# Prompt attention with its keys stored by residue class of the token

## The chip, the cores and the metric

The kernel runs on one core of a Trainium2 chip, as one program. The metric is device microseconds of one execution, the median of three runs. In what follows TensorE is also PE (its weight loads are PEld), VectorE is DVE, ScalarE is ACT, GpSimd is POOL, and SyncE, which issues most of the transfers, is SP.

## The reference, cut to what matters

One layer of a decoder runs over a prompt of 2048 tokens and over 8 samples of 4 tokens. Its attention has 8 heads of 64. Three patterns (window, dilation d) = (128, 1), (512, 4), (2048, 16) are computed for every query, each over the keys at distances 0, d, 2d, ..., window, and merged by their softmax denominators. The prompt's part is:

```python
def dilated_band_attention(q, k, v, dil, n_back):
    n = s // dil; nb = n_pad // Q_BLOCK; z = b * dil          # Q_BLOCK = 128
    qs, ks, vs = to_sub(q), to_sub(k), to_sub(v)                # sub-sequence z holds tokens z, z+d, z+2d, ...
    kb, vb = blocks_with_prev(ks), blocks_with_prev(vs)         # [previous block, own block]
    scores = jnp.einsum('znqhd,znkhd->znhqk', qb, kb) * (HEAD_DIM ** -0.5)
    dist = qi + Q_BLOCK - ki
    valid = (dist >= 0) & (dist <= n_back) & (blk * Q_BLOCK - Q_BLOCK + ki >= 0)
    scores = jnp.where(valid[None, :, None], scores, -jnp.inf)
    lse = jax.nn.logsumexp(scores, axis=-1)
    p = jnp.exp(scores - lse[..., None])
    o = jnp.einsum('znhqk,znkhd->znqhd', p, vb)
```

The rest of the layer (modulated norms, the input projection, a state-space mixer, the attention of the samples over their caches, the output projection and a gated FFN) is not touched by the change.

## The kernel before

The stages run one after another, with a barrier between them: input projection, state space, prompt attention (lines 168 to 475, from about 641 to 981 us of the span), sample attention, mixing, FFN. Everything here is about the stage of the prompt's attention, `attention_stage`.

**Tiling.** The stage has 48 steps: 16 for each pattern, pattern 1 (d = 1), then 2 (d = 4), then 3 (d = 16). A step `n` takes one block of 128 queries of one residue class modulo d, with its own block of 128 keys and, where `has_prev(n)` is true, the block before it. That is so in 15 of the 16 steps of pattern 1, in 12 of 16 of pattern 2 (four classes of four blocks each) and in none of pattern 3 (16 classes of one block). A step is two halves `i = 2n + quad` of four heads each. All values are 32-bit floats.

**Where q and k lie.** In the first 16 steps the queries and keys of 128 consecutive tokens are loaded, turned on TensorE (line 312), and moved out of the PSUM bank into `qT` (by VectorE, line 421) and `kT` (by ScalarE, line 387). Both hold the head dimension on the partitions and the 2048 tokens in order along the row. The score matmul (line 327) picks its tokens with a step:

```python
first = (b + 1 - blocks) * QB * d + z
return slice(first, first + (blocks * QB - 1) * d + 1, d)
```

so neighbouring elements read are 1, 4 or 16 floats apart. The queries are the stationary operand (weight load of 128 columns, 64 partitions), the keys the moving one (128 or 256 columns). A half has four such matmuls, each recorded as two instructions, alternating between partitions 0 to 63 and 64 to 127.

**What follows a score.** VectorE scales, adds `mask` (128 x 256, zero in the band and -1e30 outside, built once on GpSimd, lines 266 to 270) and takes the row's bound (line 436); ScalarE takes exponentials, four instructions a half (line 394); TensorE turns the probabilities (line 339), 8 blocks with a previous block and 4 without; ScalarE and VectorE move them to `probsT` (387, 421); TensorE multiplies them with the rows of `v` (line 357), whose partitions are the keys of the block in order; ScalarE copies the result (402), TensorE turns it back (365), VectorE copies it into `o` (442), and GpSimd stores `o` (274).

**What sets the order.** Each engine runs its own written list and waits on semaphores. TensorE's loop over the halves is, for half i: turn the next queries (i odd) or keys (i even) while there are any; `scores(i)`; `back` (i odd); `probs(i-2)`; `values(i-3)`. VectorE's: move out turned queries (i odd), `maxima(i)`, its share of turned probabilities of i-2, the output (i odd). ScalarE's: move out turned keys (i even), `exps(i-1)`, its share of turned probabilities of i-2, `oT_out` (i even). The turned tiles (queries, keys, probabilities) take two PSUM banks in turn, in the order `turn_order`; TensorE may fill a bank again only when the tile before in that bank has been moved out (`free_turn_bank`). SyncE loads v two steps late (`V_LATE`) into a ring of four, gated by `valued`, and at the end of its list issues the first loads of the sample stage.

## Time and profile before

| what | us |
|---|---|
| median of 3 runs | 2994.49 |
| lowest and highest run | 2991.29, 2995.83 |
| the profiled execution's own time | 2997.85 |
| its span in the trace | 2996.1 |
| granted TensorE clock, mean of that execution | 0.966 of full |

Times inside the trace are microseconds from the start of the span. Busy time is the time in which an engine has an instruction under way, and of neighbouring instructions on TensorE the ends overlap the next ones' starts, so a group's length is best read from its start to the start of the next group. A count behind a name (x8) is a count of instructions merged into one row.

### The profile page before, as it was taken

What the parts mean: (1) busy time and instruction counts of PE and PEld (TensorE: products, weight loads), DVE (VectorE), ACT (ScalarE), POOL (GpSimd) and SP (SyncE); (2) the same over time, 40 slices, a digit from 0 to 9 for tenths busy, and PEclk for the clock granted to TensorE, in tenths of its full rate; (3) what the DMA queues carried; (4) which work ended last, traced back from release to release, by engine and by line L of the source; (5) the groups of instructions that cost most, each with busy time, mean ns of one, the idle gap of its engine ahead of it and who ended that gap; (6) DMA issues with size and microseconds to landing.
All of it is one profiled execution on the core that took longest, in us unless ns stands there. A gap on an engine that the chain in (4) does not pass through costs nothing.

```text
span 2996.1 us, 40303 instructions
## 1 busy us (share of the span) xinstructions
PE 2803.8 (94%) x15949; PEld 2272.1 (76%) x15949; DVE 1316.3 (44%) x2761; ACT 997.2 (33%) x2039; POOL 414.9 (14%) x556
## 2 busy tenths in 40 slices
PE   5899997989999777999599999999999999999997
PEld 3578876767777555887488888888888888999986
DVE  6446874656556327886233322333233332333321
ACT  3112221347768325665222212222122221223210
POOL 1207675420001000000000011000110001100011
PEclk8999998999999878999799999999999999999999
DMA  7663424733113855554755545556354654545421
GB/s 274 200 191 115 133 100 155 270 113 125 70 69 129 336 213 199 190 193 148 225 168 154 186 145 175 152 158 204 121 175 146 195 174 127 170 141 155 138 88 44
DMA packets 326421, 484.21 MB, mean 162 GB/s; under 512 B 22793, under 2 KB 229897, under 8 KB 317514
## 3 DMA queue, kind: packets, MB, share of 16 engines
q1 hardware_dynamic: 307168, 355.63, 36.6%
q0 software_dynamic: 18672, 125.85, 12.2%
q8 instruction: 127, 2.08, 0.3%
q14 instruction: 60, 0.49, 0.1%
q10 hardware_dynamic: 394, 0.16, 0.0%
HBM read 392.28 MB, written 155.95 MB: 183 GB/s over the span
## 4 chain that ended last, share of the span: by engine, by line
PE 51%; DMA 0%; POOL 0%; SPq 0%; DVE 0%; issue 0%; ACT 0%; POOLq 0%; DVEq 0%; ACTq 0%
PE f_ps_f L2249 33%; PE f_ps_f L2267 17%; DMA f_raw_f<-in_w_gate_dram 0%; POOL f_y_f L2220 0%; SPq L2161 0%; ACT f_ws_f L2281 0%; DVE f_tmp_f L2319 0%; DVE f_ws_f L2309 0%; POOL out_dram L2223 0%; POOL out_dram L2225 0%; DVEq L2318 0%; POOLq L2219 0%; POOLq L2217 0%; ACTq L2133 0%
## 5 line engine op out<-in xcount | busy, mean ns | idle before, releaser
L2249 PE MATMUL f_ps_f<-f_h_f,f_ws_f 128*128 128x512 f32 (+1 forms) x5280 | 1002.5, 352 | 27.1 <-DVE f_ws_f L2309 27.1
L2249 PEld LDWEIGHTS f_ps_f<-f_h_f,f_ws_f 128*128 128x128 f32 x5280 | 860.0, 188 | 169.1 <-DVE f_ws_f L2309 27.3
L2267 PE MATMUL f_ps_f<-f_ws_f,f_aT_f 128*128 128x512 f32 x2244 | 519.2, 393 | 1.0 <-DVE f_tmp_f L2319 1.0
L2309 DVE TENSOR_TENSOR f_ws_f<-f_raw_f,f_ws_f 128x1024 fp32r<-128x1024 f32 x264 | 315.9, 1224 | 416.9 <-ACT f_ws_f L2281 416.9
L2267 PEld LDWEIGHTS f_ps_f<-f_ws_f,f_aT_f 128*128 128x128 f32 x2244 | 422.0, 188 | 97.4 <-DVE f_tmp_f L2319 1.5
L2281 ACT ACTIVATE f_ws_f<-f_raw_f 128x1024 fp32r<-128x1024 f32 x264 | 268.5, 1048 | 421.3 <-PE f_ps_f L2267 394.7
L815 PE MATMUL p_out_ps<-p_w,p_hT 128*128 128x512 f32 x1632 | 387.1, 396 | 6.0 <-DVE p_qk L1063 3.7
L815 PEld LDWEIGHTS p_out_ps<-p_w,p_hT 128*128 128x128 f32 x1632 | 306.4, 190 | 79.9 <-issue 14.1
L2332 DVE TENSOR_TENSOR f_tmp_f<-f_sl_f,f_ps_f 128x512 f32<-128x512 f32 (+1 forms) x110 | 64.6, 588 | 562.0 <-PE f_ps_f L2249 561.6
L2297 ACT ACTIVATE f_aT_f<-f_tmp_f 128x512 fp32r<-128x512 f32 (+1 forms) x110 | 60.7, 552 | 520.6 <-DVE f_tmp_f L2332 520.6
L1852 PE MATMUL c_ps_w<-c_wout,c_mT 128*128 128x512 f32 (+1 forms) x816 | 195.6, 397 | 1.9 <-ACT c_wout L1880 0.9
L1852 PEld LDWEIGHTS c_ps_w<-c_wout,c_mT 128*128 128x128 f32 (+1 forms) x816 | 147.6, 183 | 43.2 <-ACT c_wout L1880 2.5
L394 ACT ACTIVATE a_probs<-a_probs,a_o 128x256 f32<-128x256 f32 (+1 forms) x384 | 171.7, 450 | 4.5 <-DVE a_o L436 4.5
L436 DVE CUSTOM_DVE_ANT_0 a_probs<-a_s_ps,a_mask 128x256 f32<-128x256 f32 (+1 forms) x384 | 117.1, 361 | 113.6 <-issue 113.5
L2220 POOL TENSOR_TENSOR f_y_f<-f_y_f,f_tmp_f 128x512 f32<-128x512 f32 (+1 forms) x34 | 45.8, 1374 | 693.6 <-DVE f_tmp_f L2319 693.3
L327 PE MATMUL a_s_ps<-a_kT,a_qT 64*128 64x256 f32 (+1 forms) x768 | 138.9, 488 | 0.0
L2293 ACT ACTIVATE f_sl_f<-f_ps_f 128x512 f32<-128x512 f32 (+1 forms) x110 | 56.9, 518 | 201.0 <-PE f_ps_f L2249 198.0
L327 PEld LDWEIGHTS a_s_ps<-a_kT,a_qT 64*128 64x128 f32 x768 | 89.2, 271 | 24.0 <-issue 11.8
L2334 DVE TENSOR_TENSOR f_aT_f<-f_tmp_f,f_aT_f 128x512 fp32r<-128x512 f32 (+1 forms) x110 | 65.3, 593 | 68.2 <-ACT f_aT_f L2297 68.2
L357 PE MATMUL a_o_ps<-a_probsT,a_v 128*64 128x128 f32 x1200 | 86.7, 281 | 0.2 <-DVE a_probsT L421 0.2
L339 PE MATMUL a_t_ps<-ident,a_probs 128*128 128x128 f32 x600 | 84.0, 277 | 0.0
L339 PEld LDWEIGHTS a_t_ps<-ident,a_probs 128*128 128x128 f32 x600 | 66.1, 140 | 18.1 <-issue 11.7
(318 smaller groups left out, 2670.2 us busy)
## 6 DMA issues: line engine op xcount, KB each, us to landing
f_raw_f<-in_w_gate_dram SPq DMA_DIRECT2D x88, 512.0 KB, 4.1
f_raw_f<-in_w_up_dram SPq DMA_DIRECT2D x88, 512.0 KB, 5.4
f_raw_f<-in_w_down_dram SPq DMA_DIRECT2D x88, 512.0 KB, 4.1
out_dram<-in_cache_k_dram POOLq DMA_DIRECT2D x8, 4088.0 KB, 14.5
out_dram<-in_cache_v_dram POOLq DMA_DIRECT2D x8, 4088.0 KB, 14.5
p_ring<-in_w_ada_dram SPq DMA_DIRECT2D x32, 512.0 KB, 4.9
b_k<-in_cache_k_dram SPq DMA_DIRECT2D x16, 1024.0 KB
b_v<-in_cache_v_dram SPq DMA_DIRECT2D x16, 1024.0 KB
```

The costliest lines, as they stand in the source:

```text
L327: mm = pe.matmul(bank[:, at:at + blocks * QB], qT[half, pair, tokens(n, 1)], kT[half, pair, tokens(n, blocks)], start=True, stop=True)
L339: mm = pe.transpose(bank[:, c * QB:(c + 1) * QB], pr[:, n % 2, hd, b * QB:(b + 1) * QB], ident[:, :])
L357: mm = pe.matmul(o_ps[n % 2][e * HD:(e + 1) * HD, pair * QB:(pair + 1) * QB], v[:, (n - (blocks - 1 - b)) % 4, hd * HD:(hd + 1) * HD], prT ...
L394: e = act.activation(pr[:, n % 2, hd, 0:w], pr[:, n % 2, hd, 0:w], ACT.Exp, scale=-1.0, bias=o[:, n % ORING, AW + hd:AW + hd + 1], accum_o ...
L436: mx = dve.tensor_tensor_reduce(pr[:, n % 2, hd, 0:w], s_ps[quad][hd % 2][:, at:at + w], mask[:, 2 * QB - w:], -SCALE, 3e38, ALU.add, ALU. ...
L815: mm = pe.matmul(out, hT[:, n % 2, a, k, :], w[b][k][:, c * 512:(c + 1) * 512], start=(k == 0 and i == 0), stop=(k == KT - 1 and i == 2))
L1852: mm = pe.matmul(ps_w[0:r, cols], mT[:, a, k, 0:r], w_out[:, b, k, cols], start=(i == 0 and k == 0), stop=(i == 2 and k == KT - 1))
L2249: mm = pe.matmul(out, ws[:, p % SPLIT, a, k * 128:(k + 1) * 128], h2[:, y, k, c0:c1], start=(k == 0 and x == 0), stop=(k == KT - 1 and x = ...
L2267: mm = pe.matmul(ps[down_bank(b, h, j)][:, :], aT[:, a, k, at:at + 128], ws[:, p % SPLIT, y, (k % 2) * 512:(k % 2 + 1) * 512], start=(k == ...
L2281: act.activation(ws[:, p % SPLIT, 0], raw[:, p % RAW], ACT.Copy).then_inc(w_hi, 1)
L2309: dve.tensor_tensor(ws[:, p % SPLIT, 1], raw[:, p % RAW], ws[:, p % SPLIT, 0].bitcast(F32), ALU.subtract).then_inc(w_lo, 1)
L2334: dve.tensor_tensor(aT[:, 1, n, c0:c1], tmp[:, u % 2, 0:c1 - c0], aT[:, 0, n, c0:c1].bitcast(F32), ALU.subtract).then_inc(a_lo, 1)
```

## The change

`kT` goes; `kW` and `qW` come, of shape [128, pairs of heads, 16, 128]: position [z][m] holds token 16m + z, so tokens are sorted by their residue modulo 16 (`WIDE`). The keys are moved out of PSUM once, now into `kW`; the queries twice, into `qT` as before and into `qW`. Each of these moves reads the bank in order and writes neighbouring elements 128 floats apart.

The score matmul reads its keys from `kW`: `keys(...)` gives, for each block, the residue classes z, z+d, ... one after another and in each of them `run` neighbouring tokens: 16 runs of 8 in pattern 1, 4 runs of 32 in pattern 2, one run of 128 in pattern 3. So in patterns 1 and 2 the columns of a score tile are in another order than before. The masks follow: three instead of one, a memset of 768 columns and six selects on GpSimd, and VectorE waits for 7 signals rather than 3. The rows of v follow: `key_rows` loads them in the order of the keys. Queries come from `qT` with their step of 1 or 4 in patterns 1 and 2, and from `qW`, in one run, in pattern 3. Rows of the output keep their order.

```diff
--- before.py
+++ after.py
@@ -173,6 +173,7 @@
     SCALE = HD ** -0.5
     PAIRS = AW // 128
     ORING = 4
+    WIDE = max(d for _, d in DILATIONS)
     IN, V_LATE = 3, 2
 
     def has_prev(n):
@@ -185,12 +186,26 @@
         z, b = divmod(i, BLOCKS // d)
         return a[b * QB * d:(b + 1) * QB * d, :].rearrange("(n d) c -> n d c", d=d)[:, z:z + 1, :]
 
-    def tokens(n, blocks):
+    def key_rows(a, n):
         pattern, i = divmod(n, BLOCKS)
         d = DILATIONS[pattern][1]
         z, b = divmod(i, BLOCKS // d)
-        first = (b + 1 - blocks) * QB * d + z
-        return slice(first, first + (blocks * QB - 1) * d + 1, d)
+        turns = WIDE // d
+        return a[b * QB * d:(b + 1) * QB * d, :].rearrange("(m r d) c -> r m d c", r=turns, d=d)[:, :, z, :]
+
+    def queries(tensor, half, pair, n):
+        pattern, i = divmod(n, BLOCKS)
+        d = DILATIONS[pattern][1]
+        z, b = divmod(i, BLOCKS // d)
+        first = b * QB * d + z
+        return tensor[half, pair, first:first + (QB - 1) * d + 1:d]
+
+    def keys(tensor, half, pair, n, blocks):
+        pattern, i = divmod(n, BLOCKS)
+        d = DILATIONS[pattern][1]
+        z, b = divmod(i, BLOCKS // d)
+        turns, run = WIDE // d, QB * d // WIDE
+        return tensor[half, pair, z:WIDE:d, (b + 1 - blocks) * run:(b + 1) * run].rearrange("p r (x m) -> p x r m", x=blocks)
 
     def units(i):
         n, quad = divmod(i, 2)
@@ -217,13 +232,14 @@
 
     with ExitStack() as ctx:
         P = Pool_(nc, ctx)
-        mask = P.sb("a_mask", [128, 2 * QB])
+        mask = P.sb("a_mask", [128, len(DILATIONS), 2 * QB])
         gate = P.sb("a_gate", [1, 2])
         q = P.sb("a_q", [128, IN, AW])
         k = P.sb("a_k", [128, IN, AW])
         v = P.sb("a_v", [128, 4, AW])
         qT = P.sb("a_qT", [128, PAIRS, SEQ])
-        kT = P.sb("a_kT", [128, PAIRS, SEQ])
+        qW = P.sb("a_qW", [128, PAIRS, WIDE, SEQ // WIDE])
+        kW = P.sb("a_kW", [128, PAIRS, WIDE, SEQ // WIDE])
         pr = P.sb("a_probs", [128, 2, HEADS, 2 * QB])
         prT = P.sb("a_probsT", [128, 2, 2, 4 * QB])
         oT = P.sb("a_oT", [128, 2, PAIRS, QB])
@@ -252,8 +268,11 @@
             wait_turned(eng, u)
             src = turn_bank(u)
             if u[0] in ("q", "k"):
-                dst, n = qT if u[0] == "q" else kT, u[1]
-                last = move(dst[:, :, n * QB:(n + 1) * QB], src[:, :].rearrange("p (j n) -> p j n", j=PAIRS))
+                n, run = u[1], QB // WIDE
+                wide = src[:, :].rearrange("p (j m z) -> p j m z", j=PAIRS, z=WIDE)
+                if u[0] == "q":
+                    move(qT[:, :, n * QB:(n + 1) * QB], src[:, :].rearrange("p (j n) -> p j n", j=PAIRS))
+                last = move((qW if u[0] == "q" else kW)[:, :, :, n * run:(n + 1) * run].rearrange("p j z m -> p j m z"), wide)
             else:
                 i, x = u
                 if i >= 2:
@@ -263,12 +282,15 @@
 
         @block.gpsimd
         def _(pool):
-            pool.memset(mask[:, :], 0.0).then_inc(mask_made, 1)
+            pool.memset(mask[:, :, :], 0.0).then_inc(mask_made, 1)
             pool.wait_ge(mask_made, 1)
-            pool.affine_select(out=mask[:, 0:QB], in_=mask[:, 0:QB], compare_op=ALU.is_ge, fill=NEG,
-                               base=0, pattern=[[1, QB]], channel_multiplier=-1).then_inc(mask_made, 1)
-            pool.affine_select(out=mask[:, QB:], in_=mask[:, QB:], compare_op=ALU.is_ge, fill=NEG,
-                               base=0, pattern=[[-1, QB]], channel_multiplier=1).then_inc(mask_made, 1)
+            for i, (_, d) in enumerate(DILATIONS):
+                turns, run = WIDE // d, QB * d // WIDE
+                before, own = (mask[:, i, x * QB:(x + 1) * QB].rearrange("p (r m) -> p r m", r=turns) for x in range(2))
+                pool.affine_select(out=before, in_=before, compare_op=ALU.is_ge, fill=NEG, base=0, pattern=[[1, turns], [turns, run]],
+                                   channel_multiplier=-1).then_inc(mask_made, 1)
+                pool.affine_select(out=own, in_=own, compare_op=ALU.is_ge, fill=NEG, base=0, pattern=[[-1, turns], [-turns, run]],
+                                   channel_multiplier=1).then_inc(mask_made, 1)
             for n in range(STEPS):
                 pool.wait_ge(o_sb, n + 1)
                 pool.dma_start(rows(t["o"][n // BLOCKS], n), o[:, n % ORING].unsqueeze(1)).then_inc(o_stored[n % 2], 16)
@@ -289,7 +311,7 @@
                 if m >= 0:
                     if m >= 4:
                         sp.wait_ge(valued, 2 * (m - 3) + 2)
-                    sp.dma_start(v[:, m % 4].unsqueeze(1), rows(t["v_prompt"], m)).then_inc(v_loaded[m % 4], 16)
+                    sp.dma_start(v[:, m % 4], key_rows(t["v_prompt"], m)).then_inc(v_loaded[m % 4], 16)
             for n in range(S_HELD):
                 for which in range(2):
                     load_sample(sp, t, const["sample"], n, which)
@@ -324,8 +346,8 @@
                     for e in range(2):
                         bank, at, half = s_ps[quad][e], j * 2 * QB, slice(e * HD, (e + 1) * HD)
                         blocks = 2 if has_prev(n) else 1
-                        mm = pe.matmul(bank[:, at:at + blocks * QB], qT[half, pair, tokens(n, 1)], kT[half, pair, tokens(n, blocks)],
-                                       start=True, stop=True)
+                        turned_q = qW[half, pair, n % BLOCKS, :] if n >= STEPS - BLOCKS else queries(qT, half, pair, n)
+                        mm = pe.matmul(bank[:, at:at + blocks * QB], turned_q, keys(kW, half, pair, n, blocks), start=True, stop=True)
                 mm.then_inc(scored, 1)
 
             def probs(i):
@@ -433,7 +455,7 @@
                 for j in range(4):
                     hd = 4 * quad + j
                     at = (j // 2) * 2 * QB
-                    mx = dve.tensor_tensor_reduce(pr[:, n % 2, hd, 0:w], s_ps[quad][hd % 2][:, at:at + w], mask[:, 2 * QB - w:],
+                    mx = dve.tensor_tensor_reduce(pr[:, n % 2, hd, 0:w], s_ps[quad][hd % 2][:, at:at + w], mask[:, n // BLOCKS, 2 * QB - w:],
                                                   -SCALE, 3e38, ALU.add, ALU.min, o[:, n % ORING, AW + hd:AW + hd + 1])
                 mx.then_inc(masked, 1)
 
@@ -441,7 +463,7 @@
                 dve.wait_ge(oT_back, n + 1)
                 dve.tensor_copy(o[:, n % ORING, 0:AW], o_ps[n % 2][:, :]).then_inc(o_sb, 1)
 
-            dve.wait_ge(mask_made, 3)
+            dve.wait_ge(mask_made, 1 + 2 * len(DILATIONS))
             for n in range(2):
                 turned_out(dve, move, ("q", n))
             for i in range(HALVES + 4):
```

On VectorE, at the first halves of pattern 1 in which queries are moved out; `a_t_ps` is the PSUM bank of turned tiles, `a_s_ps` the scores. Before:

```order
657 L436 ISA a_o 128x1
658 L421 COPY a_qT<-a_t_ps 128x4x128
659 L432 MEMSET a_gate 1x1
660 L436 ISA a_probs,a_o<-a_s_ps,a_mask 128x256
661 L436 ISA a_o 128x1
```

After:

```order
661 L458 ISA a_o 128x1
662 L443 COPY a_qT<-a_t_ps 128x4x128
663 L443 COPY a_qW<-a_t_ps 128x4x8x16
664 L454 MEMSET a_gate 1x1
665 L458 ISA a_probs,a_o<-a_s_ps,a_mask 128x256
666 L458 ISA a_o 128x1
```

Before and after, the rows end with the first of the half's four mask instructions. A second copy, with its output scattered, now stands behind the first and ahead of the next mask-and-maximum.

On TensorE, in the middle of pattern 3; `a_s_ps` rows are the four score matmuls of a half, keys first and queries second. Before:

```order
858 L357 MATMUL a_o_ps<-a_probsT,a_v 64x128 x4
859 L327 MATMUL a_s_ps<-a_kT,a_qT 128x128 x4
860 L339 MATMUL a_t_ps<-ident,a_probs 128x128 x4
861 L357 MATMUL a_o_ps<-a_probsT,a_v 64x128 x4
862 L327 MATMUL a_s_ps<-a_kT,a_qT 128x128 x4
863 L365 MATMUL a_o_ps<-ident,a_oT 128x128 x4
```

After:

```order
858 L379 MATMUL a_o_ps<-a_probsT,a_v 64x128 x4
859 L350 MATMUL a_s_ps<-a_kW,a_qW 128x128 x4
860 L361 MATMUL a_t_ps<-ident,a_probs 128x128 x4
861 L379 MATMUL a_o_ps<-a_probsT,a_v 64x128 x4
862 L350 MATMUL a_s_ps<-a_kW,a_qW 128x128 x4
863 L387 MATMUL a_o_ps<-ident,a_oT 128x128 x4
```

Nothing moves there; the score matmuls read `a_kW` and `a_qW` instead.

On GpSimd, at the start of the stage, up to the stores of the output. Before:

```order
392 L264 UNCONDITIONAL_BRANCH
393 L266 MEMSET a_mask 128x256
394 L268 AFFINE_SELECT a_mask<-a_mask 128x128
395 L270 AFFINE_SELECT a_mask<-a_mask 128x128
396 L274 DMA scratch_o<-a_o 128x528 x48
```

After:

```order
392 L283 UNCONDITIONAL_BRANCH
393 L285 MEMSET a_mask 128x768
394 L290 AFFINE_SELECT a_mask<-a_mask 128x128
395 L292 AFFINE_SELECT a_mask<-a_mask 128x128
396 L290 AFFINE_SELECT a_mask<-a_mask 128x128
397 L292 AFFINE_SELECT a_mask<-a_mask 128x128
398 L290 AFFINE_SELECT a_mask<-a_mask 128x128
399 L292 AFFINE_SELECT a_mask<-a_mask 128x128
400 L296 DMA scratch_o<-a_o 128x528 x48
```

Four more selects stand ahead of the stores, and the memset is three times as wide.

## Rows read from the trace of the kernel before

**Rows 1.** Busy time by engine over the whole span (x: instructions).

```profile
PE 2803.8 (94%) x15949; PEld 2272.1 (76%) x15949; DVE 1316.3 (44%) x2761; ACT 997.2 (33%) x2039; POOL 414.9 (14%) x556
```

**Rows 2.** Stretches: length, busy us of PE, PEld, DVE, ACT, POOL, clock, DMA share, GB/s.

```profile
660.00:740.00 80.00, 78.94 (x764) 60.87 (x763) 55.02 (x223) 61.87 (x201) 5.48 (x10) 1.00 0.37 127
770.00:890.00 120.00, 120.00 (x939) 85.51 (x934) 66.99 (x313) 81.52 (x284) 8.11 (x15) 1.00 0.19 68
900.00:960.00 60.00, 60.00 (x518) 47.21 (x517) 36.92 (x233) 51.70 (x215) 6.25 (x12) 1.00 0.31 104
```

**Rows 3.** TensorE in pattern 1, in time: start us, us, engine, line, operation, names, instructions.

```profile
702.48 1.14 PE L327 MATMUL a_s_ps<-a_kT,a_qT 64*128 64x256 f32 x8
703.54 1.09 PE L339 MATMUL a_t_ps<-ident,a_probs 128*128 128x128 f32 x8
...
707.88 1.04 PE L339 MATMUL a_t_ps<-ident,a_probs 128*128 128x128 f32 x8
```

**Rows 4.** The same view in pattern 2, with and without previous block, and in pattern 3.

```profile
790.68 2.20 PE L327 MATMUL a_s_ps<-a_kT,a_qT 64*128 64x256 f32 x8
792.80 0.66 PE L365 MATMUL a_o_ps<-ident,a_oT 128*128 128x128 f32 x4
...
795.29 1.30 PE L327 MATMUL a_s_ps<-a_kT,a_qT 64*128 64x128 f32 x8
796.52 1.09 PE L339 MATMUL a_t_ps<-ident,a_probs 128*128 128x128 f32 x8
...
933.09 1.23 PE L327 MATMUL a_s_ps<-a_kT,a_qT 64*128 64x128 f32 x8
934.25 0.66 PE L339 MATMUL a_t_ps<-ident,a_probs 128*128 128x128 f32 x4
```

**Rows 5.** First score group of the stage: its stretch as in rows 2, then in time.

```profile
645.00:646.50 1.50, 1.50 (x10) 0.96 (x9) 0.20 (x1) 1.02 (x2) 0.00 (x0) 0.50 1.05 391
...
645.36 1.23 PE L327 MATMUL a_s_ps<-a_kT,a_qT 64*128 64x128 f32 x8
646.51 1.11 PE L312 MATMUL a_t_ps<-ident,a_q 128*128 128x128 f32 x4
```

**Rows 6.** Weight loads of the scores in pattern 1, then 2: min/median/max ns, first and last start.

```profile
L327 PEld LDWEIGHTS a_s_ps<-a_kT,a_qT x182: 182/187/187, 651.9 to 738.8; 64*128 64x128 f32 x182
...
L327 PEld LDWEIGHTS a_s_ps<-a_kT,a_qT x256: 292/307/329, 770.7 to 893.9; 64*128 64x128 f32 x128
```

**Rows 7.** ScalarE over one step of pattern 3, in time; brackets: idle before, and releaser.

```profile
965.54 0.60 ACT L387 ACTIVATE a_probsT<-a_t_ps 128x512 f32<-128x512 f32 x1 [0.72 <-PE a_t_ps L339]
...
966.63 0.39 ACT L394 ACTIVATE a_probs<-a_probs,a_o 128x128 f32<-128x128 f32 x1
...
970.64 0.60 ACT L387 ACTIVATE a_probsT<-a_t_ps 128x512 f32<-128x512 f32 x1 [0.72 <-PE a_t_ps L339]
```

**Rows 8.** VectorE in an odd half of pattern 1, ScalarE's copy of keys, in time.

```profile
706.43 0.69 DVE L421 COPY a_qT<-a_t_ps 128x512 f32<-128x512 f32 x1 [0.70 <-PE a_t_ps L312]
707.51 0.42 DVE L436 CUSTOM_DVE_ANT_0 a_probs<-a_s_ps,a_mask 128x256 f32<-128x256 f32 x1 [0.39 <-issue]
...
702.59 0.60 ACT L387 ACTIVATE a_kT<-a_t_ps 128x512 f32<-128x512 f32 x1 [1.45 <-PE a_t_ps L312]
```

**Rows 9.** VectorE operations whose output is scattered: min/median/max ns, first and last start, form.

```profile
L975 DVE COPY z_pwR<-keep_pw x32: 163/174/1286, 35.3 to 397.8; 128x16 f32<-128x16 f32 x32
...
L1392 DVE TENSOR_TENSOR y_hl<-y_ha,y_ps_v x32: 151/158/161, 526.3 to 625.1; 128x8 f32<-128x8 f32 x32
```

**Rows 10.** Start of the stage, in time: masks on GpSimd, first queries on VectorE.

```profile
638.41 0.31 POOL L266 MEMSET a_mask<- 128x256 f32 x1 [10.45 <-POOLq L73]
...
638.87 0.29 POOL L268 TENSOR_SCALAR_AFFINE_SELECT a_mask<-a_mask 128x128 f32<-128x128 f32 x1
...
642.42 0.69 DVE L421 COPY a_qT<-a_t_ps 128x512 f32<-128x512 f32 x1 [11.42 <-PE a_t_ps L312]
```

**Rows 11.** Time from issue to landing of the loads of v.

```profile
DMA to landing us min/median/max: 2.5/2.8/5.4
```

## The prediction

> **What bounds the kernel now.** I read the busy times first: TensorE works for 94% of the span [rows 1]. So an edit is worth what it takes from TensorE's list, as long as TensorE stays the last engine in its stage. The stretches of the three patterns say how near that is [rows 2]. In pattern 1 TensorE is busy 78.9 of 80 us, ScalarE 61.9, VectorE 55.0. In pattern 2 TensorE is busy all 120 us, ScalarE 81.5. In pattern 3 TensorE is busy all 60 us, ScalarE 51.7, which is 86%: near behind. The clock is granted in full in all three.
>
> Then the score matmuls in time. A group is one half: four matmuls, eight instructions. From start to next start, pattern 1 (256 columns, step 1) takes 703.54 - 702.48 = 1.06 us [rows 3]. Pattern 2 takes 792.80 - 790.68 = 2.12 us for the same 256 columns with step 4, and 796.52 - 795.29 = 1.23 us for 128 columns; pattern 3 takes 934.25 - 933.09 = 1.16 us for 128 columns with step 16 [rows 4]. So a step of four floats doubles the matmul, and one of sixteen costs no more than that. The weight loads show it as well: 187 ns with step 1, 307 ns with step 4 [rows 6].
>
> To price a dense group of 128 columns there is one row: the first group of the stage, step 1, took 646.51 - 645.36 = 1.15 us with the clock granted at 0.50, the lower of its two levels [rows 5]. At full clock that is at least 0.58 us.
>
> **Splitting a group.** In pattern 2, 128 more columns of keys cost 2.12 - 1.23 = 0.89 us, so 256 strided columns cost 1.78 and the rest, 0.34, is queries. If dense keys cost half, 256 of them cost 0.89, and pattern 1 leaves 1.06 - 0.89 = 0.17 for dense queries. A dense group of 128 columns is then 0.445 + 0.17 = 0.61 us, close to the 0.58 from the cold row. This estimate holds together, so I use it.
>
> **The change part by part.**
>
> *Pattern 2, with previous block: 12 steps, 24 groups.* Keys become dense in runs of 32, queries keep step 4: 0.89 + 0.34 = 1.23 us instead of 2.12, saving 0.89 x 24 = 21.4 us. Bound above: if the queries' step hides under the keys, the group is pattern 1's 1.06, 25.4 us in all. ScalarE is idle for 32% of this pattern [rows 2], and TensorE gives up under 20% of the 120 us shown, so TensorE stays the bound and all of it counts.
>
> *Pattern 2, without: 4 steps, 8 groups.* Either the keys pace them (0.445 + 0.34 = 0.79 us, saving 0.44) or the strided weight load does, which stays (nothing saved). I take the middle, 0.22 x 8 = 1.8 us, ends 0 and 3.5.
>
> *Pattern 3: 16 steps, 32 groups.* Both operands become dense: 1.16 to 0.61 us, 1.1 us less in a step for TensorE, so 5.1 becomes 4.0. But ScalarE's step is 970.64 - 965.54 = 5.10 us with only 0.72 us idle [rows 7]: its own work is 4.38. So ScalarE becomes the bound, and the saving is at most 0.72 a step, 11.5 us. Some of the wait (ScalarE for the turned probabilities) will stay; I take 0.65 x 16 = 10.4 us, low end 0.5 x 16 = 8. What is late next is ScalarE's list: eight exponentials, one move of `probsT`, one of `oT`.
>
> *Pattern 1: 30 groups of 256 columns, now read in runs of 8 floats.* No matmul of this trace reads such runs. The lower bound is no change: eight neighbouring floats are two steps of four, so seven of eight reads are of the dense kind. The upper bound is that they are priced as strided: 0.89 x 30 = 26.7 us more. I take the lower end: the price seems to go with the distance to the element before, and only one in eight is far. Were it exactly one in eight at the strided price, it is 0.11 x 30 = 3.3 us; that goes into the range.
>
> *The second copy of the queries, 16 times, and scattered writes.* VectorE copies a bank in 0.69 us [rows 8]. The output is now scattered by 512 bytes. Rows with scattered output are short: 16 floats in 174 ns and 8 in 158 ns [rows 9], 2 ns an element between them, against 0.69 us / 512 = 1.35 ns. So the new copy costs 0.69 to about 1.1 us. Cover: VectorE has 25 of 80 us free in pattern 1 [rows 2], 2.5 us of each step of about 8 us. Behind the copy on VectorE stands the next mask group: copies from 706.43 end at 707.8 instead of 707.1, and the group began at 707.51 [rows 8], so 0.3 us late, and its reader on ScalarE has 18 of 80 us free. TensorE waits for the bank itself when it turns the second tile of probabilities, half way through the group at 707.88 [rows 3], at 708.40. That leaves 0.6 us: the cover is gone if the second copy takes over 1.3 us, and from there each excess counts 14 times. ScalarE's scattered copy of keys replaces one of 0.60 us [rows 8], begins at 702.59, and its bank is wanted in the middle of the group at 703.54, at 704.05: cover 0.86 us more. Nothing for both, 1 us in 16 for the ends.
>
> *Start of the stage.* The memset of 0.31 us becomes about 0.9, the two selects of 0.29 us become six [rows 10]: 638.41 + 0.9 + 1.8 = 641.1 us, ahead of VectorE's first copy at 642.42. Nothing. But both first copies of queries are doubled before TensorE has anything else to do: up to 0.7 us each, I take 1 us.
>
> *Loads of v.* They land in 2.8 us, at worst 5.4 [rows 11], and are issued two steps or more ahead of use, 10 us even in a short pattern 3. Were one four times slower it would still be hidden. Nothing. The sample stage starts at the barrier and its held loads are issued three steps before it; all of it moves up.
>
> **Sum.** -21.4 - 1.8 - 10.4 + 1 = -32.6 us. Against the profiled execution, 2997.85 us, that is 2965.3; it stands 3.4 us above the median of the runs, 2994.49. On the median's scale the forecast is **2962 us**.
>
> **The Trainium skill against the rows.** The group with step 4 takes twice the dense one [rows 4]. The page "SBUF — State Buffer", section on Door 1, speaks of lines of 16 bytes, wants two hits in a line for full speed, and puts the free step at four floats. The first half agrees with the rows; the second does not, since four floats apart already costs double here. By that second half pattern 2 would gain nothing from dense keys, and the time would be that of rival 2. For runs of 8, two whole lines, the same page gives full speed, which is the end that I took.
>
> The queries' share with step 4 was 0.34 us a group by my split. The page "TensorE: Matmul & The Clock Gate", section "Part 2: What happens when you issue a matmul", has weights come through a read port of their own, so that loading them takes nothing from the running matmul; by it the 24 groups end at 1.06 us, and the sum gains 4 us more.
>
> **The rivals.**
>
> 1. *Short runs are read as strided.* Pattern 1 pays 0.89 x 30 = 26.7 us. Against: seven of eight neighbours are adjacent. For: no row shows it. Time 2962 + 26.7 = 2989. Half of it would be 2975.
> 2. *Pattern 2 keeps its time*, because something other than the step of the keys makes 2.12 us, such as the step of the queries, which stays 4. Against: 128 more columns with the same queries cost 0.89 us [rows 4]. Time 2962 + 23.2 = 2985.
> 3. *Scattered writes are slow: slower than before.* The place is pattern 1, the two banks of turned tiles. A copy of queries over 1.3 us or of keys over 1.46 us stops TensorE, once each a step. The 32.6 us are gone when both excesses make 32.6 / 14 = 2.3 us a step, that is copies of about 2.5 us, 5 ns an element. For: one of the 32 scattered copies took 1286 ns for 16 floats. Against: their median gives 2 ns at most. At 8 ns an element, copies of 4.1 us, it is 14 x (2.8 + 2.6) = 76 us lost, 3038.
> 4. *ScalarE does not keep pace in pattern 3*, its waits rise as TensorE's slack goes, and nothing is won there: 2962 + 10.4 = 2972.
>
> **How the numbers follow.** Forecast 0.72; rival 1 in full 0.06, in part 0.08; rival 2 0.05; rival 3 0.04; rival 4 0.05. The forecast's own range: best 25.4 + 3.5 + 11.5 = 40.4, giving 2954; worst 21.4 + 0 + 8 less 3.3, 1 and 1 for pattern 1, its copies and the start, 24, giving 2970. The range reaches over rival 4 and the smaller part of rival 1: 2952 to 2979. A measurement of this kernel can tell 0.2%, 6 us, from no change. Faster by more than that: the forecast, rivals 2 and 4, rival 1 in part, and half of rival 1 in full: 0.92. Same: 0.04. Slower: 0.04.
>
> **What would show it.** In the profile of the changed kernel: score groups of pattern 1 at 1.06 us (rival 1: near 1.95); of pattern 2 at 1.06 to 1.23 with and 0.79 to 1.23 without previous block (rival 2: 2.12); of pattern 3 at 0.6, with TensorE no longer busy throughout and ScalarE over 95% busy, steps of 4.4 to 4.5 us (rival 4: 5.1); copies into `a_qW` under 1.1 us, and no wait of TensorE for a move of `a_qW` or `a_kW` (rival 3: copies over 1.3 us, such waits). The attention stage ends near 948 instead of 981 us. Wrong as a whole would be a gain that appears there and is given back in a later stage.

## The result and the profile after

| kernel | median us (lowest to highest) | ratio to before, 95% interval |
|---|---|---|
| before, beside it | 2995.16 (2991.29 to 2996.67), 4 runs | |
| changed | 2968.55 (2965.76 to 2971.57), 4 runs | 0.9913 [0.9901, 0.9926] |
| changed, timed again later (before beside it then: 2994.82, 7 runs) | 2968.28 (2963.19 to 2972.59), 4 runs | 0.9917 [0.9902, 0.9932] |

The forecast was 2962, the range 2952 to 2979. The change is 0.9% faster and inside the range; it gains 26.6 us where 32.6 were forecast. The profiled execution took 2971.57 us by its own time, its span is 2969.8 us at a clock of 0.964. TensorE's share over the whole span, answering [rows 1], hardly moves; so the stage has to be read.

```profile
PE 2767.8 (93%) x15949; PEld 2257.6 (76%) x15949; DVE 1328.1 (45%) x2777; ACT 998.1 (34%) x2039; POOL 416.9 (14%) x560
```

The stretches after, with the columns of [rows 2]; the stage is shorter, so the third ends at 940:

```profile
660.00:740.00 80.00, 75.66 (x734) 58.31 (x731) 60.80 (x222) 61.42 (x193) 4.96 (x9) 1.00 0.39 121
770.00:890.00 120.00, 119.84 (x1170) 99.33 (x1166) 80.70 (x395) 98.90 (x360) 10.29 (x19) 1.00 0.24 87
900.00:940.00 40.00, 39.48 (x420) 30.02 (x420) 29.59 (x191) 40.00 (x174) 4.87 (x9) 1.00 0.43 138
```

Pattern 2 is still TensorE's (119.84 of 120 us). In pattern 3 ScalarE is now busy throughout. In pattern 1 TensorE fell from 78.94 to 75.66 of 80 us: it waits there, which I had not forecast.

TensorE in time, answering [rows 3] and [rows 4]: pattern 1, then pattern 2 with and without previous block, then pattern 3.

```profile
702.44 0.63 PE L334 MATMUL a_t_ps<-ident,a_q 128*128 128x128 f32 x4 [0.42 <-ACT a_probsT L409]
703.00 1.13 PE L350 MATMUL a_s_ps<-a_kW,a_qT 64*128 64x256 f32 x8
704.06 0.66 PE L387 MATMUL a_o_ps<-ident,a_oT 128*128 128x128 f32 x4
...
710.73 0.63 PE L334 MATMUL a_t_ps<-ident,a_q 128*128 128x128 f32 x4 [0.42 <-ACT a_probsT L409]
...
792.60 1.31 PE L350 MATMUL a_s_ps<-a_kW,a_qT 64*128 64x256 f32 x8
793.85 0.66 PE L387 MATMUL a_o_ps<-ident,a_oT 128*128 128x128 f32 x4
...
796.33 1.20 PE L350 MATMUL a_s_ps<-a_kW,a_qT 64*128 64x128 f32 x8
797.46 1.09 PE L361 MATMUL a_t_ps<-ident,a_probs 128*128 128x128 f32 x8
...
910.39 0.71 PE L350 MATMUL a_s_ps<-a_kW,a_qW 64*128 64x128 f32 x8
911.04 0.33 PE L361 MATMUL a_t_ps<-ident,a_probs 128*128 128x128 f32 x1
```

From start to next start: pattern 1 takes 1.06 us, as before, so keys in runs of 8 floats cost no more than keys in one run. Pattern 2 with previous block takes 1.25 us (2.12 before; over all 24 groups it is 1.24), without 1.13 (1.23 before). Pattern 3 takes 0.65 in the even half of a step and 0.77 in the odd one (1.16 in both before); the experiments come back to the 0.12 between them. A step of pattern 1 is 710.73 - 702.44 = 8.29 us, where it was 7.98.

I then split each profile at fixed events: the first turn of TensorE in the stage, the first score group of each pattern, the issue of the last store of `o`, and the first TensorE instruction of the sample stage. A minus is time gained, us:

| part | before | after | difference | forecast |
|---|---|---|---|---|
| first turn to first scores | 4.17 | 5.01 | +0.84 | +1 |
| pattern 1 | 118.34 | 122.00 | +3.66 | 0 |
| pattern 2 | 126.35 | 104.38 | -21.97 | -23.2 |
| pattern 3 to last store | 90.89 | 76.71 | -14.18 | -10.4 |
| the stage | 339.75 | 308.10 | -31.65 | -32.6 |
| last store to sample stage's first TensorE instruction | 9.97 | 11.45 | +1.48 | 0 |
| all else in the span | 2646.4 | 2650.2 | +3.9 | 0 |

Two opposite misses in the stage nearly cancel: 3.7 us lost in pattern 1 and 3.8 us gained in pattern 3 beyond the forecast. Another 5 us are given back outside it.

### The profile page after: what moved, and what is told of

Its sections match the earlier page's. It is cut to its first block, busy times and chain, and to the rows that moved or that the text cites. A ratio compares the mean times of both kernels' runs of the same rounds, so it can differ in the third digit from the quotient of the medians.

```text
span 2969.8 us, 40327 instructions
## 1 busy us (share of the span) xinstructions
PE 2767.8 (93%) x15949; PEld 2257.6 (76%) x15949; DVE 1328.1 (45%) x2777; ACT 998.1 (34%) x2039; POOL 416.9 (14%) x560
## 4 chain that ended last, share of the span: by engine, by line
PE 51%; DMA 0%; POOL 0%; SPq 0%; DVE 0%; issue 0%; ACT 0%; POOLq 0%; DVEq 0%; ACTq 0%
PE f_ps_f L2271 34%; PE f_ps_f L2289 17%; DMA f_raw_f<-in_w_gate_dram 0%; POOL f_y_f L2242 0%; SPq L2183 0%; ACT f_ws_f L2303 0%; DVE f_tmp_f L2341 0%; DVE f_ws_f L2331 0%; POOL out_dram L2245 0%; POOL out_dram L2247 0%; DVEq L2340 0%; POOLq L2241 0%; POOLq L2239 0%; ACTq L2155 0%
## 5 line engine op out<-in xcount | busy, mean ns | idle before, releaser
L1822 POOL DMA_DIRECT2D scratch_h2T<-c_h2T x17 | 19.0, 1116 | 420.7 <-DVE c_h2T L2067 420.7
L350 PE MATMUL a_s_ps<-a_kW,a_qT 64*128 64x256 f32 (+1 forms) x512 | 77.6, 422 | 0.0
L379 PEld LDWEIGHTS a_o_ps<-a_probsT,a_v 128*64 128x64 f32 x1200 | 63.5, 136 | 16.4 <-issue 16.0
```

The source lines that it names most:

```text
L350: mm = pe.matmul(bank[:, at:at + blocks * QB], turned_q, keys(kW, half, pair, n, blocks), start=True, stop=True)
L379: mm = pe.matmul(o_ps[n % 2][e * HD:(e + 1) * HD, pair * QB:(pair + 1) * QB], v[:, (n - (blocks - 1 - b)) % 4, hd * HD:(hd + 1) * HD], prT ...
```

## The experiments

The theories at the start. **A:** the 0.3 us a step of pattern 1 come from ScalarE's scattered move of keys, which delays what is queued behind it on ScalarE. **B:** they come from VectorE's second copy of the queries. For the groups: the strided weight load paces pattern 2 where keys are dense. The 5 us outside: scatter, or the held loads of the samples, which now come later than the stage's end wants them.

**Keys alone.** No `qW`; pattern 3 reads its queries from `qT` with step 16.

```diff
-                if u[0] == "q":
-                    move(qT[...], src[...])
-                last = move((qW if u[0] == "q" else kW)[...], wide)
+                if u[0] == "q":
+                    last = move(qT[...], src[...])
+                else:
+                    last = move(kW[...], wide)
...
-                        turned_q = qW[half, pair, n % BLOCKS, :] if n >= STEPS - BLOCKS else queries(qT, half, pair, n)
+                        turned_q = queries(qT, half, pair, n)
```

> Only the keys are sorted; qW and VectorE's second copy of the queries go, and pattern 3 reads its queries from qT with step 16 again. Theory A (in pattern 1 the scattered move of the keys on ScalarE, 1.03 us for 0.60, delays ScalarE's list and so the bank that the next queries are turned into): the step of pattern 1 stays at 8.29 us. Rival B (VectorE's second copy, 1.05 us, is what TensorE waits for): the step goes back to 7.98 us. Pattern 3: by my split of a group (0.44 us for 128 dense keys and 0.34 for strided queries) the group takes 0.79 us and ScalarE stays the bound at 4.20 us a step, so the total is within 1 us of the changed kernel, 2968; if a strided weight load paces a group of 128 columns, as the 1.14 us of pattern 2 without a previous block suggest, it takes 1.1 us, TensorE's step is 5.0 and the total is 2968 + 0.8 x 16 = 2981.

Measured 2974.99 us (2973.32 to 2978.14), ratio 0.9938 [0.9924, 0.9953]. The step of pattern 1 stayed at 8.29 to 8.30 us without any second copy: B falls. The step of pattern 3 is 4.93 us instead of 4.20, so `qW` is worth 0.73 x 16 = 11.7 us there. Without the second copy the stage's first scores come earlier, 4.32 us behind the first turn instead of 5.01. An odd half's group of pattern 3 of this kernel, TensorE in time:

```profile
919.62 1.14 PE L350 MATMUL a_s_ps<-a_kW,a_qT 64*128 64x128 f32 x8
920.69 0.66 PE L387 MATMUL a_o_ps<-ident,a_oT 128*128 128x128 f32 x4
```

Its keys are dense, and it still takes 1.07 us, where the same group of the changed kernel takes 0.77. Only the step of the queries differs: the weight load with step 16 sets the group.

**Keys moved densely.** ScalarE writes the keys in token order and pattern 1 reads them so. Patterns 2 and 3 read the addresses of the changed kernel, which hold other tokens; masks and rows of v are left as they are.

```diff
-                last = move((qW if u[0] == "q" else kW)[...], wide)
+                if u[0] == "q":
+                    last = move(qW[...], wide)
+                else:
+                    last = move(kW[:, :, n, :], src[:, :].rearrange("p (j n) -> p j n", j=PAIRS))
...
+                        turned_k = keys(kW, half, pair, n, blocks) if n >= BLOCKS else kW[half, pair, n + 1 - blocks:n + 1, :]
```

> ScalarE moves the turned keys densely, as the kernel before did; the second, scattered copy of the queries on VectorE stays. Pattern 1 reads its keys in token order. The keys of patterns 2 and 3 are other tokens than they should be, at the same addresses and in the same access pattern, and masks and rows of v are left as they are, so only times count here. Theory A: the step of pattern 1 goes back from 8.29 to 7.98 us, TensorE's wait before the turn of the queries goes, and the total falls by 15 x 0.31 = 4.6 us and some 0.4 at the start, to 2963.5. Rival B: the step stays at 8.29 and the total at 2968.5.

Measured 2962.05 us (2960.4 to 2963.43), ratio 0.9895 [0.9879, 0.9912]. The step of pattern 1 is 7.98 us again, the pattern 118.02 us instead of 122.00. The second copy of the queries is still there, and a score group of pattern 1 takes 1.06 us in both kernels, so it is not the way in which the keys are read. A holds. The two kinds of copy, changed kernel first, then this one (min/median/max ns in the first two rows; busy us and mean ns behind the bar in the last):

```profile
L443 DVE COPY a_qW<-a_t_ps x16: 1029/1046/1157, 645.1 to 753.5; 128x512 f32<-128x512 f32 x16
L409 ACT ACTIVATE a_kW<-a_t_ps x16: 1029/1032/1182, 645.2 to 757.0; 128x512 f32<-128x512 f32 x16
```

```profile
L413 ACT ACTIVATE a_kW<-a_t_ps 128x512 f32<-128x512 f32 x16 | 9.6, 597 | 32.4 <-PE a_t_ps L337 32.3
```

By its row a scattered copy of 128x512 takes 1.03 us on ScalarE and 1.05 us on VectorE, 2.0 ns an element of a row, against 0.60 and 0.69 us when dense. What a copy adds to its engine's list is read better from its start to the next start, since the rows overlap: 0.49 us for ScalarE's dense move of keys in this kernel, and 0.83 for the scattered one (707.24 to 708.07 below), 0.34 more.

```profile
701.48 0.60 ACT L413 ACTIVATE a_kW<-a_t_ps 128x512 f32<-128x512 f32 x1 [1.45 <-PE a_t_ps L337]
701.97 0.50 ACT L420 ACTIVATE a_probs<-a_probs,a_o 128x256 f32<-128x256 f32 x1
```

The way of the delay, on ScalarE in the changed kernel, in time:

```profile
707.24 1.03 ACT L409 ACTIVATE a_kW<-a_t_ps 128x512 f32<-128x512 f32 x1 [1.45 <-PE a_t_ps L334]
708.07 0.47 ACT L416 ACTIVATE a_probs<-a_probs,a_o 128x256 f32<-128x256 f32 x1
...
710.01 0.58 ACT L409 ACTIVATE a_probsT<-a_t_ps 128x512 f32<-128x512 f32 x1
```

Key move, four exponentials, then the move of the first tile of probabilities, with no pause between them. That last move frees the bank into which TensorE turns the next queries, and TensorE's row at 710.73 has waited 0.42 us for just this. The view of who waits for line 409 counts it:

```profile
  PE a_t_ps L334: 5.2, 12
```

5.2 us in 12 waits, where the pattern lost 3.7 us. Part of the wait was there before the change. From the product with v to the turn of the queries TensorE took 705.77 - 704.57 = 1.20 us before and takes 710.73 - 709.22 = 1.51 us now, 0.31 more, which is the step's loss; 12 times that is 3.7 us. Before, then after:

```profile
704.57 1.09 PE L357 MATMUL a_o_ps<-a_probsT,a_v 128*64 128x128 f32 x16
705.77 0.63 PE L312 MATMUL a_t_ps<-ident,a_q 128*128 128x128 f32 x4
...
709.22 1.09 PE L379 MATMUL a_o_ps<-a_probsT,a_v 128*64 128x128 f32 x16
```

**The first tile of an even half by VectorE.** If A holds, a shorter list for ScalarE there mends it.

```diff
     def by_act(u):
         ...
         n, quad = divmod(u[0], 2)
+        if n < BLOCKS and has_prev(n):
+            return u[1] == (0 if quad else 1)
         return u[1] == 0 if has_prev(n) else quad == 0
```

> The changed kernel with one thing swapped: in the even halves of pattern 1 VectorE, not ScalarE, moves out the first of the two tiles of turned probabilities, and ScalarE the second. The bank in which the next queries are turned is the first tile's. Theory A: VectorE is done with its mask group at 701.4 us in the trace where ScalarE comes to the tile at 701.7, so the bank is free 0.3 us earlier, the step shrinks from 8.29 to 8.0 us and the total to 2964. Rival (TensorE waits for something else at that place, or the exponentials are late either way): no change, 2968.5, or later, if VectorE's list is now the long one.

Measured 2963.95 us (2961.88 to 2966.21), ratio 0.9900 [0.9886, 0.9915]. The step fell to 8.10 us, the pattern to 119.55. The same place in this kernel:

```profile
706.26 0.42 DVE L460 CUSTOM_DVE_ANT_0 a_probs<-a_s_ps,a_mask 128x256 f32<-128x256 f32 x1 [1.01 <-issue]
...
707.64 0.69 DVE L445 COPY a_probsT<-a_t_ps 128x512 f32<-128x512 f32 x1
...
708.47 0.63 PE L336 MATMUL a_t_ps<-ident,a_q 128*128 128x128 f32 x4 [0.22 <-DVE a_probsT L445]
```

The wait is halved and now ends with VectorE's move of the tile. The second copy is not what holds that up: VectorE stood idle for 1.01 us ahead of this half's four mask instructions, which run from 706.26 to the move at 707.64.

The medians of these three kernels don't settle A against B by themselves: the changed kernel's one run beside them took 2962.82 us, and the intervals of the ratios overlap its own. The step does, which is the same to 0.01 us in all three profiles of the changed kernel.

**The stage's end.** The held loads of the samples are issued in pattern 2 instead of at the end of SyncE's list.

```diff
+                if n in (BLOCKS + 6, BLOCKS + 10):
+                    load_sample(sp, t, const["sample"], 0, (n - BLOCKS) // 10)
...
-            for n in range(S_HELD):
-                for which in range(2):
-                    load_sample(sp, t, const["sample"], n, which)
```

> The changed kernel with the eight transfers that fill the held buffers of the sample stage (2 x 2.3 MB) issued in pattern 2, where the transfer engines are busy a fifth of the time, and not behind the last load of v. In three executions of the changed kernel and its variants 11.2 to 11.5 us pass from the issue of the last store of the stage to the first instruction of TensorE in the next, in the kernel before 10.0, and in one with a slower pattern 3 10.2. Theory (the last stores queue behind these loads, and with a shorter pattern 3 more of the loads is still to come): the stretch shrinks to about 6 us and the total by 5 us, to 2963 beside 2968.5 for the changed kernel in its first job (2958 beside 2963 in the last). Rival (the barrier itself takes that long): the stretch stays 11.4 us.

Measured 2966.34 us (2965.5 to 2966.53), ratio 0.9907 [0.9892, 0.9922]. From the last store to the sample stage 8.97 us pass, where the changed kernel had 11.45, 11.34 and 12.20 in its three profiles and the one before 9.97 and 10.06. The last store of `o` shows where the time goes. From issue to landing, in the kernel before, the changed kernel and this one:

```profile
scratch_o<-a_o POOLq DMA_DIRECT2D x1, 264.0 KB, 3.3
...
scratch_o<-a_o POOLq DMA_DIRECT2D x1, 264.0 KB, 4.7
...
scratch_o<-a_o POOLq DMA_DIRECT2D x1, 264.0 KB, 2.3
```

In each of the three 6.7 us are left from its landing to the sample stage, so the whole difference is the store, slowed by the held loads beside it. The other two profiles of the changed kernel have 4.5 and 5.4 us, the kernel with the longer steps of pattern 3 (keys alone) 3.6 and 10.24 us to the sample stage. So the 1.5 us given back are real: three steps of pattern 3 are 2.7 us shorter, and more of the loads is still to come when the last store is issued. The 6 us hoped for were wrong, because 6.7 of them do not depend on the loads; what they are stays open. The median is 2.2 us below that of the changed kernel, which was not timed beside it.

**Shorter runs.** Keys by residue class modulo 64: pattern 1 reads runs of 2 floats, pattern 2 of 8, pattern 3 of 32. Masks and rows of v follow.

```diff
+    KW = 64
...
-        turns, run = WIDE // d, QB * d // WIDE
-        return tensor[half, pair, z:WIDE:d, ...
+        turns, run = KW // d, QB * d // KW
+        return tensor[half, pair, z:KW:d, ...
```

> Keys sorted by their class modulo 64 and not 16, masks and rows of v with them: pattern 1 reads runs of 2 floats (8 bytes) with 128 bytes between them, pattern 2 runs of 8, pattern 3 runs of 32. This prices short runs beyond rival 1 of the prediction. If a float costs by its distance to the one before, half of the 256 are far and a group of pattern 1 takes 0.17 + 0.89 x 1.5 = 1.51 us; if two floats in one 16-byte line are enough for full speed, it takes 1.06 us, as with runs of 8. Pattern 2's group with previous block stays 1.24 us by either, pattern 3's 0.65.

Measured 2969.3 us (one run). The group of pattern 1 takes 707.83 - 706.76 = 1.07 us with every second float far from the one before:

```profile
706.76 1.14 PE L355 MATMUL a_s_ps<-a_kW,a_qT 64*128 64x256 f32 x8
707.83 0.44 PE L366 MATMUL a_t_ps<-ident,a_probs 128*128 128x128 f32 x2
```

By the distance to the element before, as I had argued, it would be 1.51 us. Two neighbours are enough for 1.07 us, against 1.06 in runs of 8.

**Dense queries in pattern 2.** It reads `qW` as pattern 3 does, so the queries there are those of other tokens; the work is the same.

```diff
-                        turned_q = qW[half, pair, n % BLOCKS, :] if n >= STEPS - BLOCKS else ...
+                        turned_q = qW[half, pair, n % BLOCKS, :] if n >= BLOCKS else ...
```

> Pattern 2 reads its queries densely from qW, at the address of pattern 3's, which are other queries than it should read, so only times count. This takes the queries' step of four away alone. By my split of a group (strided queries 0.34 us, dense 0.17) a group with previous block takes 1.06 us for 1.24, one without 0.65 for 1.14, and pattern 2 shrinks by 24 x 0.18 + 8 x 0.49 = 8.2 us, from 104.4 to 96.2. If the queries' loads hide under the keys with 256 columns, 1.24 stays, and it is 3.9 us.

Measured 2957.0 us (one run). Pattern 2 with, then without previous block:

```profile
787.17 1.14 PE L350 MATMUL a_s_ps<-a_kW,a_qW 64*128 64x256 f32 x8
788.24 0.66 PE L387 MATMUL a_o_ps<-ident,a_oT 128*128 128x128 f32 x4
...
790.72 0.72 PE L350 MATMUL a_s_ps<-a_kW,a_qW 64*128 64x128 f32 x8
791.37 0.44 PE L361 MATMUL a_t_ps<-ident,a_probs 128*128 128x128 f32 x2
```

1.07 and 0.65 us instead of 1.25 and 1.13: a strided weight load costs 0.18 us a group under 256 columns of keys and 0.48 us under 128. In an odd half without previous block the dense group takes 0.77 us, as in pattern 3, so 0.36 are won there. The pattern falls by 7.65 us, from 104.38 to 96.73, where 8.2 were expected: the eight groups gain 0.43 us each in the mean and not 0.49. A version that computes the reference would need a third layout of the queries for it; no run has one.

**Which engine sets 4.20 us in pattern 3.** Two kernels take work from one engine each. The best version, below, gives every second of ScalarE's moves of probabilities to VectorE. I expected 4.0 us of it, TensorE's own list; the step stays 4.20, with ScalarE busy for 36.97 us of its stretch (columns as in [rows 2]):

```profile
900.00:940.00 40.00, 38.83 (x411) 29.58 (x408) 31.16 (x186) 36.97 (x164) 5.40 (x10) 1.00 0.36 121
```

And ScalarE's copy of the output there, in time:

```profile
905.54 0.60 ACT L427 ACTIVATE a_oT<-a_o_ps 128x512 f32<-128x512 f32 x1 [0.53 <-PE a_o_ps L382]
```

The other takes work from TensorE: half of the matmuls that turn the output back are left out in pattern 3, and so the output is left unturned in half of its columns there.

```diff
-                for j in range(PAIRS):
+                for j in range(PAIRS if n < STEPS - BLOCKS else PAIRS // 2):
                     mm = pe.transpose(o_ps[n % 2]...
```

> The changed kernel with two of the four matmuls left out that turn the output of a step back, in pattern 3 alone (16 steps); half of the output columns of pattern 3 are left as the product with v had them. TensorE has 0.33 us less to do in each step, ScalarE and VectorE the same. If TensorE sets the step of 4.20 us alone, it falls to 3.87 us, pattern 3 by 5.3 us. If ScalarE's list sets it as well (it was busy 39.99 of 40 us), the step stays at 4.20 us to within 0.03.

Measured 2963.3 us (one run); the step is 4.04 us, between the two expectations. ScalarE in this kernel, one step in time:

```profile
912.95 0.61 ACT L409 ACTIVATE a_probsT<-a_t_ps 128x512 f32<-128x512 f32 x1
913.42 0.61 ACT L424 ACTIVATE a_oT<-a_o_ps 128x512 f32<-128x512 f32 x1
...
916.98 0.61 ACT L409 ACTIVATE a_probsT<-a_t_ps 128x512 f32<-128x512 f32 x1
```

The next move follows 0.47 us behind. In the changed kernel 0.60 us pass at the same place, with no pause shown:

```profile
911.73 0.60 ACT L409 ACTIVATE a_probsT<-a_t_ps 128x512 f32<-128x512 f32 x1
912.33 0.60 ACT L424 ACTIVATE a_oT<-a_o_ps 128x512 f32<-128x512 f32 x1
...
915.93 0.60 ACT L409 ACTIVATE a_probsT<-a_t_ps 128x512 f32<-128x512 f32 x1
```

So ScalarE's list is 4.04 us long. "Busy 40.00 of 40" on ScalarE held 0.16 us a step in which it stood still between instructions whose rows overlap.

TensorE's own list is 4.20 - 0.12 = 4.08 us, just above, and 5.10 - 2 x (1.16 - 0.65) gives the same. The 0.12 us are a wait at a hand-over. Its rows in the changed kernel:

```profile
912.21 0.71 PE L350 MATMUL a_s_ps<-a_kW,a_qW 64*128 64x128 f32 x8
912.98 0.42 PEld L387 LDWEIGHTS a_o_ps<-ident,a_oT 128*128 128x128 f32 x4 [0.24 <-ACT a_oT L424]
```

ScalarE can copy the output (`a_oT`, 912.33) only when TensorE has made the product with v, and TensorE turns it back behind the next scores. Those took 1.16 us before and covered the copy of 0.60 us. Now the dense group takes 0.65 us in the even half and 0.77 here, because TensorE waits for the copy. That is also why a shorter list for ScalarE did nothing: in the best version the copy still waits for TensorE's product, 0.53 us in its row above, and the step holds the same 0.77.

**Both kernels once more, for the scatter.** Kernel before, unchanged:

> The kernel before once more, for its profile: how much its stretches outside the attention stage scatter. If the scatter is what made the first pair of profiles differ by 26.3 us where the stage alone differed by 31.7, the stage takes 339.75 us again to within 0.3 us, while its start (641.19 us in the first profile) and the time from the sample stage's first instruction to the end of the span (2005.2 us) each move by 1 to 4 us. If instead the changed kernel really loses in later stages, both stay within 0.5 us.

The changed kernel, profiled with the first experiments, and timed and profiled with the last:

> The changed kernel once more, unedited. Its first profiled execution began the attention stage 2.0 us later than that of the kernel before (643.2 against 641.2 us), in code that both share, and its last stage was 1.2 us longer. If that is scatter between executions, the start moves here by a microsecond or more; if the change causes it, the start is 643.2 again within 0.3 us. Inside the stage both say the same: a step of pattern 1 in 8.29 us, a group of scores with a previous block in pattern 2 in 1.24 us, a step of pattern 3 in 4.20 us.

> The changed kernel once more, timed in the same job as the best version. By the stage's own figure, 31.7 us shorter, the median should lie 29 to 32 us under that of the kernel before; by the first measurement, 26.6 us.

Before gave 2994.01 us (one run, span 2992.2); the changed kernel 2962.82 (one run, span 2961.0) and 2968.28 (four, span 2967.6). The stage took 338.47 us before, 307.92 and 307.94 after. From the sample stage to the end of the span it took 2005.2 and 2000.9 us before; 2007.0, 2000.1 and 2004.4 after: the same kernel moves by 7 us there. The mean spans, 2994.2 of two and 2966.1 of three, differ by 28.0 us; the stage by 31.1, less 1.6 at its end makes 29.5. The spread of the changed kernel outside the stage is as large as what is missing.

**The best version.** The edits of the two experiments on moves and held loads, and one more:

```diff
+        if n >= STEPS - BLOCKS:
+            return quad == 0 and n % 2 == 0
```

> Three edits to the changed kernel together: the held loads in pattern 2 as in e4, the two moves of the even halves of pattern 1 swapped as in e3 (2.4 us less in its stage), and in pattern 3 every second of ScalarE's moves of turned probabilities given to VectorE, which is 73% busy there while ScalarE never idles. The last takes 0.3 us a step from ScalarE, so the step goes from 4.20 to 4.0 us, which is what TensorE's own list takes, 3 us in all. Sum: 5 + 2.4 + 3 = 10 us under the changed kernel, 2953 beside 2963 for that kernel in the last job. If TensorE or the wait for VectorE decides in pattern 3, its part is nothing and the total 2956.

> The best version once more: held loads of the samples issued in pattern 2, VectorE moves the first tile of probabilities in even halves of pattern 1, every second move of probabilities in pattern 3 is VectorE's. Its profile had 2.4 us less in pattern 1, 2.4 us less at the barrier and 0.5 less in pattern 3 than the changed kernel, so 4 to 6 us less in the median. If its 2959.16 us owed itself to the state of that job, the two medians lie within 2 us.

Measured 2959.16 us (2957.37 to 2962.93), ratio 0.9887 [0.9870, 0.9903], and later 2960.97 (2959.27 to 2962.06), ratio 0.9895 [0.9878, 0.9911], beside 2968.28 for the changed kernel timed with it. It is faster than the kernel before both times, and 7.3 us faster than the changed one, which was timed beside it the second time. That is less than the 10 us expected at first. Its profiles have 2.4 to 2.6 us less in pattern 1, 0.5 less in pattern 3 and, against the three profiles of the changed kernel, 2.2 to 3.2 less at the end of the stage. So the move of probabilities in pattern 3 bought 0.5 us of its 3.

## Why the prediction was right, and where it was not

- **What bounds it:** right. TensorE is still busy for 119.84 of 120 us of pattern 2 and has the longest list in pattern 3, so what was taken from it came off the stage: 31.7 us of 32.6 in sum.
- **Pattern 2 with previous block:** -21.4 forecast. 24 x (2.12 - 1.24) = 21.1. The size was right for a wrong reason: my split gave the queries 0.34 us of every group as a share added to the keys. The runs show that the weight load costs 0.18 under 256 columns and 0.48 under 128, which is no fixed share.
- **Pattern 2 without:** -1.8 forecast, 8 x (1.23 - 1.13) = 0.8. Of the two ends, the weight load's was the right one; 0.79 us for the group came from the split and never showed.
- **Pattern 3:** -10.4 forecast, 14.2 measured. The mechanism, ScalarE as the bound, was not what happened: TensorE's list of 4.08 us and its wait of 0.12 for the copy of the output make the step of 4.20, ScalarE's list at 4.04 is just behind. The step that failed is "its own work is 4.38": I took the step of 5.10 less the one idle time that the row showed, and small pauses without a row stayed in. The cap of 11.5 us was therefore none. TensorE's side was sized nearly right: 0.61 forecast for a group, 0.65 measured, 4.0 for its list, 4.08 measured. The wait for the copy of the output was not thought of.
- **Pattern 1, the reads:** right, 1.06 us, and rival 1 is out. The reason given, that the price goes with the distance to the element before, is wrong (runs of 2).
- **Pattern 1, the copies:** the step that failed is "Nothing for both". The copies were priced well (1.1 us at most, measured 1.03 and 1.05). The cover was judged wrongly: for ScalarE I asked only when TensorE wants the bank that the key move holds. What decided was the move of probabilities, five instructions further down ScalarE's list, whose bank TensorE wants next. This was the mechanism of rival 3, but it sets in below the 1.46 us that I gave for the copy of keys: 1.03 us were enough, 0.34 more on ScalarE's list than before.
- **Start:** +1 forecast, +0.84 measured. The masks were made by 643.2 us, the first copy of queries started at 644.45. Without the second copy the start took 4.32 us, so the copy makes 0.69 of it.
- **Rivals 2 and 4:** out, by groups of 1.25 us and steps of 4.20.
- **The stage's end:** "all of it moves up" failed by 1.5 us. The held loads are issued a fixed number of steps ahead, and the steps became shorter, so the last store takes 4.5 to 5.4 us to land instead of 3.3.
- **Small slips in the numbers:** the chances named for a time beyond 6 us faster add up to 0.93, not 0.92. Loads of v four times slower would take 11.2 us, more than the 10 us given for hiding them; neither changes the forecast.
- **The sum:** the stage predicts 29.5 us with its end, the two timed medians show 26.6 with intervals of about 20 to 30. The remaining 3 us lie within the scatter of the other stages by the profiles here; whether some of it is caused by the change stays open. That the total came within 6 us of the gain forecast is in part luck: the misses of pattern 1 and pattern 3 have opposite signs.

**The two rules that the prediction cited.** The groups show 2.12 us for keys with step 4 [rows 4], 1.07 for runs of 2 and 1.06 for runs of 8. The page "SBUF — State Buffer" of the Trainium skill, section on Door 1, asks for two hits in a line of 16 bytes: with runs of 2 the trace agrees. The free step of four floats, which it also states, is not what this kernel shows.

A weight load with step 4 costs the running group 0.18 us under 256 columns. The group takes 1.24 us, longer than with dense weights (1.06) and longer than the strided weight loads alone set it (1.13, under 128 columns). The page "TensorE: Matmul & The Clock Gate" of the Trainium skill, section "Part 2: What happens when you issue a matmul", gives the weights a read port of their own, so that loading them takes nothing from the running matmul; the trace does not agree for strided weights, and the group of 1.06 us did not come. Why the two together take longer than either stays open.

## What to carry to other kernels

Price a slower instruction by all that is queued behind it on its engine until the first tile for which the bound engine waits, not by its own output alone. Take the length of an engine's list from instruction starts in a stretch where it never waits, or bound it from both sides: step less shown idle time is too long. When a group of matmuls becomes shorter, look for the copy on another engine that it covered. And when steps become shorter, look again at every load issued a fixed number of steps ahead.

## What the runs showed of the hardware

- Moving operand of a 32-bit matmul, group of four with 256 columns: step 4 takes 2.12 us, runs of 2 floats 1.07, runs of 8 1.06. Two neighbours suffice here; I had expected the price to grow with the number of jumps.
- Stationary operand with step 4 or 16: a group of four with 128 dense columns takes 1.13 or 1.07 us, with dense weights 0.65 (even half) or 0.77 (odd half, with a wait). The weight load sets it, and under 256 columns it still costs 0.18 us.
- Copies of 128x512 floats out of PSUM with neighbouring elements written 512 bytes apart: 1.03 us on ScalarE, 1.05 us on VectorE, 2.0 ns an element; dense 0.60 and 0.69.
- A store of 264 KB issued some 10 us behind loads of 4.6 MB landed after 4.5 to 5.4 us; with these loads issued in pattern 2 instead it landed after 2.3 us.
